# Adding the squares in pairs on Pool instead of VectorE at the entry of the feed-forward stages

## The reference

```python
def rmsnorm(x, g):
    xf = x.astype(jnp.float32)
    y = xf * lax.rsqrt(jnp.mean(xf * xf, -1, keepdims=True) + EPS)
    return (y * g.astype(jnp.float32)).astype(x.dtype)

def macaron_half_ffn(x, pre_g, post_g, w_gate, w_up, w_down):
    h = rmsnorm(x, pre_g)
    h = (jax.nn.silu(h @ w_gate) * (h @ w_up)) @ w_down
    return x + 0.5 * rmsnorm(h, post_g)
```

## Time and profile before

| what | value |
|---|---|
| median of 3 runs | 3581.78 us |
| lowest, highest | 3574.05, 3582.15 us |
| profiled execution, its own time | 3582.93 us |
| its span, first to last instruction | 3581.1 us |
| mean granted TensorE clock | 0.925 |
| PE busy | 3283.6 us, 92% |
| DVE busy | 1808.7 us, 51% |
| ACT busy | 1526.3 us, 43% |
| POOL busy | 912.4 us, 25% |
| chain that ended last, by engine | PE 81%, DVE 9%, ACT 5%, issue 3%, POOL 1% |

### The profile page before, as it was taken

One profiled execution on the slowest core, in us unless ns is written; L12 is line 12 of the kernel. 1 busy time (PEld: TensorE's weight loads), 2 busy tenths in 40 slices (PEclk: granted clock), 3 DMA queues, 4 the chain that ended last, 5 costly groups with the idle time before them and its releaser, 6 DMA issues.

```text
span 3581.1 us, 63633 instructions
## 1 busy us (share of the span) xinstructions
PE 3283.6 (92%) x27126; PEld 3135.0 (88%) x27126; DVE 1808.7 (51%) x3157; ACT 1526.3 (43%) x2540; POOL 912.4 (25%) x474
## 2 busy tenths in 40 slices
PE   9998999989788999989969999999899979977998
PEld 9996999987678999988858899899799979975898
DVE  5446555558565454474655344544435454454443
ACT  5444444434124444356454344443334443432442
POOL 3221222322342323212202122222122222220222
PEclk9988999989898999989979999999899989986899
DMA  6541454544003555533414345354224524520353
GB/s 229 187 150 59 147 184 164 184 164 147 31 3 129 178 171 188 172 111 116 148 42 152 116 163 188 132 176 138 89 83 154 176 100 160 177 83 18 109 175 118
DMA packets 133385, 484.43 MB, mean 135 GB/s; under 512 B 14959, under 2 KB 17151, under 8 KB 132399
## 3 DMA queue, kind: packets, MB, share of 16 engines
q1 hardware_dynamic: 131120, 470.25, 38.9%
q0 software_dynamic: 1984, 10.12, 0.9%
HBM read 479.27 MB, written 1.05 MB: 134 GB/s over the span
## 4 chain that ended last, share of the span: by engine, by line
PE 81%; DVE 9%; ACT 5%; issue 3%; POOL 1%; DMA 0%; DVEq 0%; POOLq 0%; ACTq 0%
PE ps L178 80%; ACT hi L175 1%; DVE lo L158 1%; ACT arena L175 1%; PE ps L186 1%; DVE arena L158 1%; POOL small L158 1%; DVE tmp L166 1%; DVE yT L166 1%; DVE arena L166 1%; ACT L175 1%; DVE small L172 1%; ACT xT L175 0%; ACT hh L175 0%; DVE hl L158 0%
## 5 line engine op out<-in xcount | busy, mean ns | idle before, releaser
L178 PE MATMUL ps<-hh,lo 128*128 128x256 f32 (+1 forms) x4624 | 1342.8, 290 | 0.0
L178 PE MATMUL ps<-hh,hi 128*128 128x256 f32 (+1 forms) x4336 | 1273.9, 294 | 74.5 <-DVE hl L166 33.2
L178 PE MATMUL ps<-hl,hi 128*128 128x256 f32 (+1 forms) x4336 | 1261.1, 291 | 0.0
L158 POOL TENSOR_TENSOR lo<-raw,hi 128x1024 fp32r<-128x1024 f32 x271 | 687.3, 2536 | 1893.2 <-ACT hi L175 1893.1
L175 ACT ACTIVATE hi<-raw 128x1024 fp32r<-128x1024 f32 x814 | 852.5, 1051 | 462.8 <-PE ps L178 341.9
L158 DVE TENSOR_TENSOR lo<-raw,hi 128x1024 fp32r<-128x1024 f32 x543 | 699.0, 1290 | 603.3 <-ACT hi L175 582.5
L178 PEld LDWEIGHTS ps<-hh,hi 128*128 128x128 f32 x4336 | 851.1, 196 | 91.1 <-DVE hl L166 24.2
L178 PEld LDWEIGHTS ps<-hh,lo 128*128 128x128 f32 x4624 | 904.5, 196 | 0.0
L178 PEld LDWEIGHTS ps<-hl,hi 128*128 128x128 f32 x4336 | 849.2, 196 | 0.2
L178 PE MATMUL ps<-hfh,lo 128*128 128x256 f32 (+1 forms) x1760 | 499.7, 284 | 0.0
L178 PE MATMUL ps<-hfh,hi 128*128 128x256 f32 (+1 forms) x1520 | 431.2, 284 | 0.0
(11 more groups left out here) (351 smaller groups left out, 3859.6 us busy)
## 6 DMA issues: line engine op xcount, KB each, us to landing
raw<-in_l_ffn_w_gate SPq DMA_DIRECT2D x88, 512.0 KB, 3.5
raw<-in_l_ffn_w_up SPq DMA_DIRECT2D x88, 512.0 KB, 4.0
raw<-in_l_ffn_w_down SPq DMA_DIRECT2D x88, 512.0 KB, 4.2
raw<-in_g SPq DMA_DIRECT2D x88, 512.0 KB, 3.3
raw<-in_u SPq DMA_DIRECT2D x88, 512.0 KB, 3.3
raw<-in_d SPq DMA_DIRECT2D x88, 512.0 KB, 3.3
raw<-in_ffn_w_gate SPq DMA_DIRECT2D x44, 512.0 KB, 4.3
raw<-in_ffn_w_up SPq DMA_DIRECT2D x44, 512.0 KB, 4.3
```

Source lines behind the costliest of these rows:

```text
L158: return self.e.tensor_tensor(o, a, b, op)
L178: return self.e.matmul(o, a, b, start=first, stop=final, skip_group_check=loose)
```

## The change

The four additions move from DVE's program to POOL's. In DVE's program they stood behind the last `hl` of the entry and ahead of `Norm.variance`; in POOL's they stand where the entry's part begins, ahead of `W.lo_pool(pool, u + 8)` and of `Norm.power`. The waits for the squares and the semaphore that PE waits for are the same.

```diff
         if self.start:
             K.W.lo(dve, 4)
             K.enter.all(dve)
+        self.norm.variance(dve, then=(self.var, self.after))
+
+    def pool(self, pool):
+        K, T = self.K, self.T
+        self.prev.upd_pool(pool)
         for k in (0, 2, 4, 6):
-            dve.wait_ge(*self.sq(k + 1))
-            dve.tt(K.sq[:, k, 0:T], K.sq[:, k, 0:T], K.sq[:, k + 1, 0:T], ALU.add).then_inc(self.pr.h, 1)
-        self.norm.variance(dve, then=(self.var, self.after))
-
-    def pool(self, pool):
-        self.prev.upd_pool(pool)
+            pool.wait_ge(*self.sq(k + 1))
+            pool.tt(K.sq[:, k, 0:T], K.sq[:, k, 0:T], K.sq[:, k + 1, 0:T], ALU.add).then_inc(self.pr.h, 1)
```

More of the change, by code:

```diff
@@ L712, in dve @@
             K.enter.all(dve)
-        for k in (0, 2, 4, 6):
-            dve.wait_ge(*self.sq(k + 1))
-            dve.tt(K.sq[:, k, 0:T], K.sq[:, k, 0:T], K.sq[:, k + 1, 0:T], ALU.add).then_inc(self.pr.h, 1)
         self.norm.variance(dve, then=(self.var, self.after))
     def pool(self, pool):
+        K, T = self.K, self.T
         self.prev.upd_pool(pool)
+        for k in (0, 2, 4, 6):
+            pool.wait_ge(*self.sq(k + 1))
+            pool.tt(K.sq[:, k, 0:T], K.sq[:, k, 0:T], K.sq[:, k + 1, 0:T], ALU.add).then_inc(self.pr.h, 1)
     def scale(self, act):
```

## The result

| | before | changed |
|---|---|---|
| median | 3581.78 us (7 runs, 3574.05 to 3588.80) | 3591.47 us (7 runs, 3585.68 to 3593.53) |
| ratio of the runs, 95% interval | | 1.0028 [1.0018, 1.0038] |
| span of the profiled execution | 3581.1 us | 3590.7 us |
| mean granted clock | 0.925 | 0.924 |
| DVE busy | 1808.7 us | 1801.8 us |

The kernel became slower by 0.28%, some 10 us. The move itself is plain in the busy times: DVE does 7 us less, POOL 29 us more. What matters is two places.

The account below looks back on a forecast made before the run. PE was taken to bound the kernel, busy 92% of the span. Stage 0's 6.6 us (4.6 + 2.0), stage 15's 2.3 and 0 elsewhere gave 8.9 us, a median of 3590.7 us; the 8-in-10 range was 3583 to 3597.

Parts of the forecast that it names:

- Stage 0, the stop: In stage 0 POOL's additions delay unit 2's low part to 19.7, so PE stands still for 4.6 us.
- Stage 0, the clock: After the new stop in stage 0 PE runs at a lowered clock, costing 2.0 us, between 1.7 and 3.0.
- Stage 15: POOL's additions hold DVE by turns, 0.6 us each, so the first hl and PE come 2.3 us later.
- The other six: Stages 2, 3, 5, 11, 13 and 17: additions hold DVE up to 0.6 us each, hidden by PE's backlog; loss 0.
- The Trainium skill's rule: Overlapping POOL additions fully block DVE instructions with two SBUF inputs; stage 15 would cost 2.9 us instead of 2.3.
- (b): Rival: in five entries DVE's chain is held longer than PE's lead, about 1.8 us each; 3600 us; chance 0.06.
- (d): Rival: the additions were on the path, gaining up to 2.2 us in stages 2, 3 and 11; chance 0.03.
- (c): Rival: stage 15 gains 1.3 us because POOL's low part no longer holds the first hl; 3587 us; chance 0.10.
- (e): Rival: the stage 0 stop does not happen, something else having held PE; 2.3 us left, 3584 us; chance 0.03.
- (a): Rival: stage 0's clock costs 3.0 us, not 2.0, and some later dips lengthen; 3593 to 3596 us; chance 0.21.

Follow-up runs that it names:

- e1_fix0: The changed kernel, but in stage 0 POOL makes unit 2's low part ahead of the additions; 3583.01 us against 3583.18 for the kernel before, ratio 1.0002.
- e2_only0: The kernel before with only stage 0's additions moved to POOL; 3588.12 us against 3583.18, ratio 1.0017.
- e3_only15: The kernel before with only stage 15's additions moved to POOL; 3583.75 us against 3583.18, ratio 1.0006.
- e4_others: The kernel before with the additions of stages 2, 3, 5, 11, 13 and 17 moved to POOL; 3577.41 us against 3583.18, ratio 0.9995.
- e7_fourfold: Only stages 2, 3, 5, 11, 13 and 17 on POOL, each addition made four times; 3583.97 us against 3582.66 for the kernel before, ratio 1.0009.
- e8_best: The kernel before, with DVE making unit 4's low part earlier in stage 0 and POOL waiting for DVE's first hl in stage 15; 3577.70 us against 3582.66, ratio 0.9986.

## Why the prediction was right

The forecast was 3590.7, a loss of 8.9 us; the median came out at 3591.47, 9.7 above that of before. By its own steps:

- **Stage 0, the stop.** Foreseen 4.6 us. Measured 4.41 idle, and 20.19 - 15.50 = 4.69 from the last product of unit 1 to the first of unit 2. The low part of unit 3 took 1.22 us undisturbed, to 15.18. The four additions took 14.79 + 3.04 - 15.18 = 2.65 us past it, where 0.6 + 3 x 0.69 = 2.7 was worked out. Undoing the order undoes it (e1_fix0), and the order alone makes it (e2_only0).
- **Stage 0, the clock.** Foreseen 2.0 between bounds of 1.7 and 3.0; measured 2.9 by the window (6 us at 0.51), 2.7 by the products. This term was too small by 0.7 to 0.9. The prediction placed the price by the length of the stop, between a short one that cost 1.7 and a long one that cost 3.0. That step is not borne out: stops of about 1.5 us cost 0, 1.7 and 2.8 in three profiles. That the measured value lies within the bounds is in part luck.
- **Stage 15.** Foreseen 2.3; the first `hl` came 1.9 later. Of the parts, the turns cost 3.30 - 1.88 = 1.4 for three additions, 0.47 each and not 0.6; the fourth was free, as said; the low part cost 3.96 - 1.79 = 2.2 among the rotary additions, and before it had cost the eight `hl` 5.10 - 3.39 = 1.7 (the prediction read 1.9 and 2.35, with nearly the same difference). So 1.4 + 0.5 is the 1.9. What the prediction did not have is what PE's clock made of it. Between the first product and the sums PE made up some: it is late by 2960.66 - 2951.31 = 9.35 us at the one and 2974.62 - 2966.13 = 8.5 at the other, with a mean clock of 0.60 over the first 6 us (2960 to 2966) instead of 0.50. Behind the sums it lost time again, in the second stretch at a low clock. In e3_only15, where this entry alone was moved, the two come to a span 2.1 us longer. So the 2.3 is nearly right at the end, but by 1.9 us and changes of the clock that it had put at nothing, which is luck; by the sums of the stage the late start is worth 1 us.
- **The other six.** Foreseen 0, held for up to 0.6 each; measured 0.48 each and no new PE wait (e4_others: ratio 0.9995). The cover was right, and larger than needed (e7_fourfold).
- **The Trainium skill's rule** (SBUF — State Buffer, "Who interferes with whom"), by which the second to issue fully blocks, agrees in kind with the held `hl`: the one at 400.01 ends at 400.97, behind POOL's addition, which ends at 400.69. In size a turn costs less than the rule's full span, for the `hl` ends 0.28 us behind the addition, though it takes 0.48 by itself. So the sum by the rule, four full additions in stage 15, was too high: three additions of 0.75 would hold DVE for 2.25 and held it for 1.4.

Of the rivals, (b) and (d) are shown wrong by e4_others, (c) by e3_only15, (e) by e2_only0. (a), the dear clock, is what happened for its first half, a price of 2.7 to 2.9 instead of 2.0. Its other half, dips further on that grow, doesn't show up to stage 11, where PE's delay is 2284.25 - 2276.70 = 7.55 us after 7.6 at stage 2; it does show behind the sums of stage 15 (0.57 where it was 1.00). Of the 9.6 us between the two spans, 0.55 lay there before the stop in stage 0 and is not the change's, some 7 are that stop and its clock, and 2.1 are what e3_only15 gives for stage 15.

## What to carry to other kernels

Before moving a step to an engine with room, write down that engine's program at each place and ask what stands behind the step: here an addition that waits for late squares was put ahead of a weight's low part, which was done at 14.56 before and at 20.14 now, and the busy share of 25% said nothing of it. Look at the first stage and at stages with another order of arrival by themselves; six of eight entries did not notice the move, and the other two made the loss that the traces show. The price of a stop of PE is the stop plus the clock behind it, here 4.4 + 2.9 us and 2.8 + 1.7 us. The second part can't be read from the stop's length: behind a stop of about 1.5 us at one place it was 0, 1.7 or 2.8 us in different profiles.

## What was not expected of the hardware

Runs of one and the same kernel spread over 14 us (the kernel before, 33 runs beside e1_fix0: 3573.46 to 3587.34), and the profiles show two places where such a difference comes from. The six-entries kernel was profiled at a span of 3575.6 us, 5.5 below the kernel before, with the same instructions in stages 0 and 1. In stage 0 its sums start 0.8 us later (21.57 against 20.75) and the first product of stage 1 0.7 us earlier (219.10 against 219.81), the low clock behind the short stop being absent. In stage 1 it gains 4.6 us more (386.41 against 391.74 at the first product of stage 2). The windows of a stretch of that stage, of the kernel before and of e4_others:

```profile
224.00:340.00 116.00, 104.19 (x802) 94.58 (x801) 68.67 (x160) 54.78 (x131) 19.85 (x9) 0.90 0.32 109
```

```profile
224.00:340.00 116.00, 102.76 (x821) 92.86 (x820) 69.34 (x159) 55.62 (x133) 20.52 (x9) 0.94 0.34 110
```

The granted clock is 0.94 against 0.90, and 821 products fit where 802 did (a few of them because this kernel is 0.7 us ahead at the start). This is a stage in which PE stops often and shortly, and it seems that whether a stop brings the clock down differs from run to run; that was not tried by itself. The profile of e8_best too gains 2 us in this stage, where neither of its edits acts. It means that a single profile can be some 5 us off in this kernel for no reason in the change, and that the 1 to 2 us of stage 15 can be read only from rows of that stage, or from a profile that is level with the other one up to it.

The other surprise is that a POOL that is never free holds DVE by no more than 0.5 us a tile, as in the rows of e7_fourfold: two engines on the shared path take turns, and the operations that read PSUM fill the others' turns.
